# Expert weights of a 16-expert MoE trunk loaded in longer runs: four neighbouring matrix rows per partition for w_gate and w_up, two for w_down

## The reference

```
aff = softmax(h @ w_router); top_aff, top_idx = top_k(aff over tokens, cap = 32)
xs  = h[top_idx]                                   # 32 tokens per expert and stream
hid = silu(xs @ w_gate[e]) * (xs @ w_up[e])        # w_gate[e], w_up[e]: 1024 x 1024
ys  = (hid @ w_down[e]) * top_aff                  # w_down[e]: 1024 x 1024, 16 experts
y   = scatter-add of ys;  x = layer_norm(ALPHA * x + g2 * y)
```

## Time and profile before

| what | value |
|---|---|
| time, median of 3 runs | 1913.62 us (1913.56 to 1915.73) |
| the profiled execution: span from first to last instruction | 1912.5 us |
| matmuls (PE), share of the span | 82% |
| weight loads (PEld) | 41% |
| DVE / ACT / POOL | 26% / 20% / 4% |
| moved by DMA | 529.01 MB, mean 277 GB/s |
| mean granted TensorE clock | 0.908 of full speed |

### The profile page before, as it was taken

One profiled execution on the slowest core, in us unless ns is written; L12 is line 12 of the kernel. 1 busy time (PEld: TensorE's weight loads), 2 busy tenths in 40 slices (PEclk: granted clock), 3 DMA queues, 4 the chain that ended last, 5 costly groups with the idle time before them and its releaser, 6 DMA issues.

```text
span 1912.5 us, 21336 instructions
## 1 busy us (share of the span) xinstructions
PE 1559.2 (82%) x8780; PEld 783.9 (41%) x8780; DVE 495.3 (26%) x1063; ACT 389.5 (20%) x877; POOL 84.9 (4%) x169
## 2 busy tenths in 40 slices
PE   5999999999979988778787799999866666666664
PEld 1544457888544522122222264578542322222221
DVE  0125775333440001010010344865320000000002
ACT  1313674222122200000000132753220000000000
POOL 1000000000000000000000010000000000000000
PEclk8999999999989999999999999999987767676767
DMA  9445713225258999999999721056769999999994
GB/s 377 154 171 245 289 40 99 98 86 186 109 204 340 396 394 400 393 403 392 403 400 391 275 65 39 1 159 214 286 238 401 406 402 405 402 406 402 406 402 184
DMA packets 151408, 529.01 MB, mean 277 GB/s; under 512 B 12800, under 2 KB 15120, under 8 KB 145168
## 3 DMA queue, kind: packets, MB, share of 16 engines
q1 hardware_dynamic: 143536, 510.44, 69.4%
q0 software_dynamic: 7232, 16.76, 2.8%
q10 hardware_dynamic: 544, 0.45, 0.1%
HBM read 520.17 MB, written 1.15 MB: 273 GB/s over the span
## 4 chain that ended last, share of the span: by engine, by line
PE 52%; DMA 37%; DVE 6%; SPq 4%; ACT 1%; issue 1%; ACTq 0%; POOL 0%; DVEq 0%
PE psum L412 48%; DMA ring<-in_w_up 17%; DMA ring<-in_w_down 15%; SPq L850 4%; PE psum L458 3%; DMA ring<-in_w_gate 2%; DMA ring<-in_w_in 2%; DVE small L1418 1%; DMA ring<-in_w_ada 1%; DVE PR L1438 1%; DVE X L1450 0%; DVE X L1449 0%; ACT hT L987 0%; DVE psum L1416 0%; DVE stats L1539 0%
## 5 line engine op out<-in xcount | busy, mean ns | idle before, releaser
L412 PE MATMUL psum<-ring,A 128*32 128x256 f32 (+2 forms) x4704 | 721.1, 547 | 254.6 <-DMA ring<-in_w_up 87.4
L412 PEld LDWEIGHTS psum<-ring,A 128*32 128x32 f32 (+2 forms) x4704 | 235.2, 139 | 713.4 <-issue 280.1
L412 PE MATMUL psum<-ring_r,h_hi 128*128 128x512 f32 x576 | 179.9, 394 | 5.8 <-DVE h_lo L1592 5.8
L1552 DVE TENSOR_TENSOR A<-A,psum 128x512 f32<-128x512 f32 (+1 forms) x32 | 17.7, 554 | 625.4 <-PE psum L412 625.4
L412 PE MATMUL psum<-ring,hT 128*128 128x512 f32 (+2 forms) x512 | 170.2, 486 | 10.7 <-DMA ring<-in_w_in 5.3
L412 PEld LDWEIGHTS psum<-ring_r,h_hi 128*128 128x128 f32 x576 | 109.5, 190 | 29.5 <-issue 6.6
L1199 ACT ACTIVATE A<-psum 128x512 f32<-128x512 f32 (+1 forms) x32 | 15.7, 491 | 519.0 <-PE psum L412 519.0
L412 PEld LDWEIGHTS psum<-ring,hT 128*128 128x128 f32 x512 | 85.6, 192 | 82.0 <-issue 79.2
L412 PE MATMUL psum<-ring_r,h_lo 128*128 128x512 f32 x288 | 113.1, 393 | 0.0
L346 POOL DMA_DIRECT2D B<-A x120 | 58.9, 497 | 951.2 <-DVE A L1568 950.2
L1592 DVE TENSOR_TENSOR ring_r<-ring,ring_r 128x2048 fp32r<-128x2048 f32 (+2 forms) x36 | 73.7, 2053 | 93.2 <-ACT ring_r L1118 93.0
(11 more groups left out here) (168 smaller groups left out, 1202.9 us busy)
## 6 DMA issues: line engine op xcount, KB each, us to landing
ring<-in_w_down SPq DMA_DIRECT2D x128, 1024.0 KB, 18.5
ring<-in_w_gate SPq DMA_DIRECT2D x124, 1024.0 KB, 18.7
ring<-in_w_up SPq DMA_DIRECT2D x124, 1024.0 KB, 19.1
ring<-in_w_ada SPq DMA_DIRECT2D x48, 1024.0 KB, 9.9
ring<-in_w_in SPq DMA_DIRECT2D x36, 1024.0 KB, 5.0
ring<-in_w_out SPq DMA_DIRECT2D x8, 1024.0 KB, 6.2
ring<-in_w_branch SPq DMA_DIRECT2D x8, 768.0 KB, 4.4
B<-A POOLq DMA_DIRECT2D x60, 64.0 KB, 5.8
```

Source lines behind the costliest of these rows:

```text
L412: return nc.tensor.matmul(o, a, b, start=start, stop=stop, skip_group_check=True)
L1552: V_.tensor_tensor(hid[:, e % 2, 0:Wd], sil[:, e % 2, 0:Wd], psum[:, b, 0:Wd], ALU.mult) \
```

## The change

Two layouts change, and with them everything that has to agree with them.

w_gate and w_up are loaded 512 matrix rows at a time. Partition p takes the four neighbouring rows 4p to 4p+3, so that each partition reads one run of 16 KB. Such a piece is 2 MB and takes two neighbouring ring slots (`wide_piece`); both are freed together, after PE has used all of it. w_down stays in 1 MB pieces of 256 rows, but partition p takes rows 2p and 2p+1, one run of 8 KB. The four early pieces of 1 MB become two of 2 MB in the same places.

A product over the channels must now pair the right channels. The gather therefore reads the columns of X with a step of four elements (`group_cols(k, 4)`), and `turn_hidden` reads the hidden values with a step of two. ACT's scale and shift have to stand in the same order, which is what the new tile `modquad` holds: `ada_rows` makes it by 16 small products on PE, and ACT copies it.

```diff
+        def row_groups(m, j):
+
+            return m.rearrange("(p j) n -> p j n", j=j)
+
+        def group_cols(k, j):
+
+            return slice(P * j * (k // j) + k % j, P * j * (k // j) + P * j, j)
...
+            def wide_piece(src, *shape):
+
+                if len(pieces) % 2:
+                    pieces.append(None)
+                    freed.append(freed[len(freed) - RING])
+                n = len(pieces)
+                both = ring[:, n % RING:n % RING + 2, :].rearrange("p a b -> p (a b)")
+                pieces.append((part(both, 0, *shape), src))
+                stream.append((*pieces[n], n, None))
+                pieces.append(None)
+                freed.extend([None, None])
+                wide.add(n)
+                loads[n % RING] += 1
+                pe.wait_ge(slot_filled[n % RING], 16 * loads[n % RING])
+                return n, pieces[n][0]
...
                 b = begin(("adaR", l), bank=TURN_BANK)
+                for j in range(4):
+                    for h in range(4):
+                        mm(psum[32 * h:32 * h + 32, b, P + j:P + 32:4], ident[:, j::4],
+                           modcol[:, l, :, 8 * SH2 + h:8 * SC2 + 8:4])
...
-                                ins = mm(psum[:, b, at:at + w], X[:, 2 * s + i, k * P:(k + 1) * P],
+                                ins = mm(psum[:, b, at:at + w], X[:, 2 * s + i, group_cols(k, 4)],
...
-                    for kp in range(4):
+                    for kp in range(2):
                         for at, (b, w) in enumerate(((bg, w_gate), (bu, w_up))):
-                            src = [w[l, e, kp * 256:kp * 256 + 256, :]]
-                            if e == 0 and kp < 2:
-                                n, v = None, early_piece(l, 2 * kp + at, src, 2, D)
+                            src = row_groups(w[l, e, kp * 512:kp * 512 + 512, :], 4)
+                            if e == 0 and kp == 0:
+                                n, v = None, early_piece(l, at, src, 4, D)
                             else:
-                                n, v = piece(src, 2, D)
-                            for k in (2 * kp, 2 * kp + 1):
+                                n, v = wide_piece(src, 4, D)
+                            for k in range(4 * kp, 4 * kp + 4):
...
-                    transposes(("HT", l, e), [hid[:, e % 2, j * P:(j + 1) * P] for j in range(Wd // P)])
+                    transposes(("HT", l, e), [hid[:, e % 2, group_cols(j, 2)] for j in range(Wd // P)])
...
-                        n, v = piece([w_down[l, e, kp * 256:kp * 256 + 256, :]], 2, D)
+                        n, v = piece(row_groups(w_down[l, e, kp * 256:kp * 256 + 256, :], 2), 2, D)
...
                 if n >= RING:
                     sp.wait_ge(*freed[n - RING])
+                    if n in wide and freed[n + 1 - RING] != freed[n - RING]:
+                        sp.wait_ge(*freed[n + 1 - RING])
```

More of the change, by code:

```diff
@@ L106, in trunk @@
         mod_rows = sb("mod_rows", [96, P])
+        modquad = sb("modquad", [P, DEPTH, 2, 2, KT])
         wr = sb("wr", [P, KT, EXPERTS])
@@ L194, in trunk @@
         mod_cols = sem("mod_cols")
+        modquad_ready = sem("modquad_ready")
         part_in = sem("part_in")
         parts = [0]
-        early_in = [sem(f"early_in{i}") for i in range(4)]
+        early_in = [sem(f"early_in{i}") for i in (0, 1)]
         split_high = sem("split_high")
@@ L238, in trunk @@
         stream, gates_done = [], {}
-        early = [(A, 8192), (A, 10240), (B, 0), (B, 2048)]
+        early = [(A, 8192), (B, 0)]
+        wide = set()
         frees, loads = [0] * RING, [0] * RING
@@ L737, in into @@
                                 drained(pe, ("XS", l, part, k0))
-                    for kp in range(4):
+                    for kp in range(2):
                         for at, (b, w) in enumerate(((bg, w_gate), (bu, w_up))):
-                            src = [w[l, e, kp * 256:kp * 256 + 256, :]]
-                            if e == 0 and kp < 2:
-                                n, v = None, early_piece(l, 2 * kp + at, src, 2, D)
-                            else:
-                                n, v = piece(src, 2, D)
-                            for k in (2 * kp, 2 * kp + 1):
+                            src = row_groups(w[l, e, kp * 512:kp * 512 + 512, :], 4)
+                            if e == 0 and kp == 0:
+                                n, v = None, early_piece(l, at, src, 4, D)
+                            else:
+                                n, v = wide_piece(src, 4, D)
+                            for k in range(4 * kp, 4 * kp + 4):
                                 for g in range(G):
                                     ins = mm(psum[g * M:(g + 1) * M, b, 0:Wd], xsT[:, k, e * M:(e + 1) * M],
-                                             v[:, k % 2, g * Wd:(g + 1) * Wd], k == 0, k == KT - 1)
-                            if kp == 3:
+                                             v[:, k % 4, g * Wd:(g + 1) * Wd], k == 0, k == KT - 1)
+                            if kp == 1:
                                 free(n, event=end(ins, b))
+                                freed[n + 1] = freed[n]
                             elif n is not None:
                                 free(n, ins)
+                                freed[n + 1] = freed[n]
                 def turn_hidden(e):
                     pe.wait_ge(hid_ready, EXPERTS * l + e + 1)
-                    transposes(("HT", l, e), [hid[:, e % 2, j * P:(j + 1) * P] for j in range(Wd // P)])
+                    transposes(("HT", l, e), [hid[:, e % 2, group_cols(j, 2)] for j in range(Wd // P)])
                 def down(e):
@@ L841, in _ @@
                     sp.wait_ge(*after)
-                    sp.dma_start(dst, src[0].rearrange("(k p) n -> p k n", p=P)).then_inc(early_in[n], 16)
+                    sp.dma_start(dst, src).then_inc(early_in[n], 16)
                     continue
@@ L977, in ada_hook @@
                         act.wait_ge(mod_stored, 16 * due["rows"])
+                    nc.scalar.copy(modquad[:, due["rows"], :, :, :],
+                                   psum[:, b, P:P + 32].rearrange("p (s w k) -> p s w k", s=2, w=2)) \
+                        .then_inc(modquad_ready, 1)
                     nc.scalar.copy(mod_rows[:, :], psum[0:96, b, 0:P]).then_inc(bank_drained[b], 1)
@@ L1182, in gathered @@
                                                            ACT.Identity,
-                                                           scale=modcol[:, l, s, 8 * SC2 + k:8 * SC2 + k + 1],
-                                                           bias=modcol[:, l, s, 8 * SH2 + k:8 * SH2 + k + 1])
+                                                           scale=modquad[:, l, s, 1, k:k + 1],
+                                                           bias=modquad[:, l, s, 0, k:k + 1])
                                 at += w
@@ L1189, in _ @@
                     ada_hook("routed")
+                act.wait_ge(modquad_ready, l + 1)
                 gathered(0)
```

## The result

| | before | changed |
|---|---|---|
| time, median of 5 runs | 1913.62 us (1912.20 to 1915.73) | 1923.11 us (1917.22 to 1923.52) |
| ratio, 95% interval | | 1.0040 (1.0027 to 1.0052) |
| span of the profiled execution | 1912.5 us | 1914.9 us, its own time 1917.22 |

The kernel became slower, by 9.5 us of the medians, where 31 us less had been forecast. The time lies outside the range. Timed again later, the changed kernel gave 1922.75 us and a ratio of 1.0051 (1.0038 to 1.0063).

A forecast was written before the change was run, and what follows sets the result against it. DMA was taken to bound the kernel, its engines never idle in both layers' expert plateaus. Sum: 1913.6 - 37.4 + 1.7 + 0.9 + 1 + 2 + 0.3 = 1882.1 us; range 1872 to 1905.

The forecast's parts named there:

- The strided reads: Gather's weight loads at a step of four: likeliest cost nothing, records staying near 116 ns; at worst each record doubles.
- Rival B: Strided loads double gather records, PE bounds layer 0's gather experts: 27 us, 1909 us; half the slowdown 1893; chance 0.15.
- What the stream carries beside weights: In the expert weight stream, POOL's moves above all: 2.0 us for each expert, taken as unchanged.
- rival D: Longer packets also shorten the 2.0 us per expert beside the weights, by 0.3 us for 30 experts: 1873 us; chance 0.08.
- The value of long runs: Expert weight stream: w_gate and w_up gain 13.7 us, w_down 5.0 us for each layer; 37.4 us for two layers.
- net sum: Whole kernel: gain of 37.4 us less costs 1.7, 0.9, 1, 2 and 0.3, giving 1882.1 us from 1913.6.
- The line through three windows: DMA packet times at 2, 4 and 8 KB: 75.0 ns per 2 KB plus 10 ns a packet; 16 KB gives 430 GB/s.
- Rival C: 16 KB runs in the weight stream are cut: to 8 KB 1891 us, to 4 KB 1909 us; chance 0.11.
- Rival A: Sixteen engines reading 16 KB each get less: slower than before, 1929 us or more, plateaus under 407 GB/s; chance 0.08.
- the 410 that were to be the sign of being right: Both layers' expert plateaus were to show 410 to 425 GB/s with POOL's moves, 425 or more without.
- The costs of pairs and small products: First stream issues later by 1.7 and 0.9 us, paired slots 1, small products 2, transposes and copy 0.3: 5.9 us.
- PE's reserve: Experts with a gather: PE needs 29.3 us while the stream brings 12 MB in 31.4 us, 2 us to spare.

The follow-up runs named there:

- e5: Changed kernel with rows of every matrix, gather and hidden values as before, keeping 2 MB pieces, paired slots and small products: 1915.77 us, 1.0007 against the kernel before.
- e1: Changed kernel with the gather reading X without a step, so wrong channels are paired: 1891.69 us, ratio 0.9885 against the kernel before.

## Why the prediction was wrong, point by point

**The strided reads: "I take nothing for the likeliest" failed.** This step decides the sign. The reason given, that a matmul of 128 columns at 116 ns leaves the load room, holds for a load of 64 lines (122 ns a record) and not for one of 128 (237 ns). Rival B had this mechanism and its size almost right: 7.4 us for a gather of layer 0 (measured 15.20 - 7.41 = 7.8 inside the experts, 15.20 - 9.95 = 5.25 for the first, which was slower before already), an expert of 36.7 us on PE (37.1), together 27 us. Measured were 27 us on the short runs and 30 to 32 on the long ones. B's sum comes closer than its terms: 7.4, 3.7 and 16 us stand against 5.0, 2.4 and 18.8.

In traces: the stream of layer 0 takes 500.5 us in the changed kernel and, with the plain gather, 18.8 less. Its first issue there is at 577.66 and its last piece lands at 1059.34 us. To this come 15.20 - 10.18 = 5.0 us for the first gather of layer 0, 7.73 - 5.30 = 2.4 for that of layer 1, and 1.3 that neither the forecast nor B had: the first early product of layer 1 takes 3.23 us and not 1.93. The granted clock over it is 0.59, near the lower level of 1.2 GHz, where it was 1.00 before, the level of 2.4. This product takes 3.2 to 3.6 us in each of the five profiles with a step of three or more and 1.93 in all nine others, so it goes with the slow gather that PE has just done there. The next two rows show it, of the changed kernel and of the kernel before.

```profile
1418.54 3.23 PE L439 MATMUL psum<-A 128*32 128x256 f32 x32 [1.79 <-ACT A L1218]
```

```profile
1404.00 1.93 PE L412 MATMUL psum<-A 128*32 128x256 f32 x32 [1.80 <-ACT A L1180]
```

Together this makes 27.5 us, and the two spans differ by 1914.9 - 1888.8 = 26.1 us. The rest of the 30 to 32 between the medians is left open above. The rule that I cited for B, in the Trainium skill's "Advanced Engine Details and Errata", section "SBUF Cachelines", asks for at least two hits on a line, and the traces agree: a step of two, the last that has them throughout, takes 7.81 us against 7.41, a step of three 11.36 and a step of four 15.20.

B had 0.15 of the chance, and that was too little: the nearest row showed a load without a step only, and the rule that I had before me spoke for B.

**What the stream carries beside weights: "I leave as it is" failed as well.** I looked at one direction only (rival D, longer packets shorten these 2.0 us per expert); it went the other way. The moves' data cost the kernel 32.1 us beside packets of 4 KB and 42.5 beside 16 and 8 KB (by the streams 32.7 and 42.7), with 8 KB between. So about 10 us of the gain were lost there. This is shown by taking the data away; why a move disturbs more is not. The moves of 1 KB, which also land later the longer the weight packets are, say only that it is not a matter of the moves' own data; no run here tests a cause.

**The value of long runs was right within the noise, and its net sum by some luck.** The line through three windows of the earlier trace rows gave 430 GB/s for 16 KB and 423 for 8 KB. Undisturbed stretches show 421 for 8 KB alone and 426 for the mix, which by the line is 428 (two thirds at 2.439 us per MB, one third at 2.479). With small moves the long runs bring 32.4 us, where the forecast's net sum was 31.5. But the costs in it were 1.3 us and not 5.9 (next point), so the runs themselves brought about 33.7 of 37.4: two misses of some 4 us cancel, of which only the one in the costs is clear of the noise. w_down alone brought 9.4 of 10.0. Rival C falls, for the packets went whole. Rival A falls by the 426 GB/s of the stretch without moves; the plateau of layer 0, 407 GB/s, lies below the 410 that were to be the sign of being right and at A's border, for the moves are in it. The other rule that I cited, three cycles of overhead for a packet (the Trainium skill, "DMA: Bandwidth & Descriptors", "Why small descriptors are slow (HBM only)"), would by the estimate have given 14 us, and the runs side with the rows.

**The costs of pairs and small products were too high.** I took 5.9 us for five terms; e5 has them all and lies 1.3 us above. The small products, forecast 2 us with a bound of 4.3, take 0.67 us for each 32 records, at 180.03 us in layer 0's attention as at 662.87. The first issue of layer 0 stands 583.20 - 555.66 - 15.20 = 12.3 us behind the end of the first gather, before it was 10.6 (558.61 + 9.95 to 579.18): 1.7 us later, as said. In layer 1 it is 2.2 us later instead of 0.9 (first issue at 1425.29): 0.9 of it is the wider slot, as said, and 1.3 the slower early product from above.

**PE's reserve was as small as said, and that decided.** The 2 us that PE had to spare with a gather in an expert were worked out rightly (29.3 against 31.4). A cost of 7.8 us meets that and leaves 5.7 for each of three experts, 17 us. The stream with the plain gather took 481.7 / 15 = 32.1 us for 12 MB and not 31.4, which leaves 5.0, 15 us; its own difference was 18.8, and these last 2 to 4 us are not explained.

Sum by the runs: 32.4 us less by long runs with their small costs in them and 10.4 more by the moves, which is the 22.0 less of the plain gather taken apart, then 27.5 more by the gather's rows. That is 5.5 us more, beside spans that are 2.4 and 4.9 us longer than that of before. The medians say 8 to 10, and the difference is what has no trace.

## What to carry to other kernels

A longer run in DRAM forces a step on whoever reads the data against it; work out how many 16-byte lines each 128-value weight load opens. In the five steps measured here for float32, two was the last that cost next to nothing. Here that meant runs of 8 KB with a step of two, 17 to 20 us below the kernel before, instead of 16 KB with a step of four, 8 to 10 above. And when the packets of a saturated stream get longer, price the small transfers beside it anew: here they took back a third of the gain.

## What the runs showed of the hardware that was not expected

- A float32 weight load of 128 columns costs about 1.85 ns for each new line of 16 bytes: 177 ns at a step of three, 237 at four, 242 at eight, while 64 lines add 6 ns to the 116 of a record.
- The 6.2 MB that the small moves leave out would take 15 us at 408 GB/s, yet they cost 32.1 us beside packets of 4 KB and 42.5 beside those of 16 and 8 KB. The windows with and without a move show 368 and 426 GB/s in e1, 370 and 409 in the kernel before.
- Behind the slow gather of layer 1 the granted clock was 0.59 and the next product took 3.23 us, behind the plain one 1.00 and 1.93 us.
- Runs of 16 KB bring only 6.1 us more than 8 KB even with small moves (64.5 and 58.4 below), and 2.1 to 4.6 us with full ones, which is within the noise: most of what a long run had to give here was had at 8 KB.
